# An expert's rows 129 to 192 as 32-row pieces in native fp32 on four column tiles, or as a second tile of 128 rows

## What is computed

```python
logits = (h @ w_router).astype(jnp.float32)
top_logit, top_e = lax.top_k(logits, TOP_K)
gates = jax.nn.softmax(top_logit, axis=-1)
...
def swiglu(h, w1, w3, w2):
    return (jax.nn.silu(h @ w1) * (h @ w3)) @ w2
...
yb = lax.map(expert_block, (xb, block_e)).reshape(n_rows, D)
y = jax.ops.segment_sum(yb * row_gate[:, None], row_tok, num_segments=T + 1)
```

## Time and profile before

| | |
|---|---|
| median of 3 runs | 2439.51 us (2437.66 to 2441.33) |
| profiled execution | 2438.57 us |
| its span | 2436.7 us |
| mean granted TensorE clock | 0.951 |
| TensorE matmul busy | 2242.2 us, 92% |
| VectorE, ScalarE, GpSimd busy | 1483.8, 1089.2, 342.9 us |
| DMA | 512.63 MB, mean 210 GB/s |

### The profile page before, as it was taken

The page is one execution under the profiler, slowest core; times in us unless marked ns, Lnnn a source line. Parts: engine busy times, 40 slices in busy tenths (PEclk is TensorE's granted clock), DMA queues, the critical chain, the costliest instruction groups (busy, mean ns, idle before and its releaser), DMA issues.

```text
span 2436.7 us, 29275 instructions
## 1 busy us (share of the span) xinstructions
PE 2242.2 (92%) x10996; PEld 1824.1 (75%) x10997; DVE 1483.8 (61%) x1330; ACT 1089.2 (45%) x1066; POOL 342.9 (14%) x211
## 2 busy tenths in 40 slices
PE   7999979999996998599899999999999999999990
PEld 4866757887875886578788888888878788888770
DVE  3456565534458444489445454458999995544986
ACT  4145433221323222577334343347777774434761
POOL 0000117888742000100000000000000000000004
PEclk8989989999998998599999999999999999999995
DMA  7420164544431222299554555549999996455963
GB/s 302 183 84 1 51 263 172 185 177 173 172 121 69 104 86 104 84 387 378 221 190 178 188 211 188 199 172 366 365 392 374 383 368 247 173 189 187 360 227 139
DMA packets 76170, 512.63 MB, mean 210 GB/s; under 512 B 8240, under 2 KB 8368, under 8 KB 19024
## 3 DMA queue, kind: packets, MB, share of 16 engines
q1 hardware_dynamic: 61344, 442.46, 47.7%
q0 software_dynamic: 14768, 69.35, 7.8%
HBM read 482.41 MB, written 29.36 MB: 210 GB/s over the span
## 4 chain that ended last, share of the span: by engine, by line
PE 88%; DVE 6%; ACT 2%; DMA 2%; issue 1%; POOL 0%; SPq 0%; POOLq 0%; DVEq 0%; ACTq 0%
PE ps L1509 26%; PE ps L1511 26%; PE ps L1510 26%; PE ps L543 2%; PE ps L498 2%; PE ps L554 2%; PE ps L1778 1%; DMA raw<-w_mod 1%; PE ps L1550 1%; PE ps L502 1%; DVE xz L1149 0%; PE ps L1721 0%; DVE rstd L1143 0%; DVE zf L1480 0%; DVE zf L1485 0%
## 5 line engine op out<-in xcount | busy, mean ns | idle before, releaser
L1509 PE MATMUL ps<-ah,hi 128*128 128x512 f32 x688 | 272.2, 396 | 19.5 <-DVE al L1116 12.9
L1510 PE MATMUL ps<-al,hi 128*128 128x512 f32 x688 | 270.4, 393 | 0.0
L1511 PE MATMUL ps<-ah,lo 128*128 128x512 f32 x688 | 270.2, 393 | 0.0
L1332 DVE TENSOR_TENSOR lob<-raw,hib 128x2048 fp32r<-128x2048 f32 x112 | 251.6, 2282 | 12.3 <-DMA dispatched_x<-ht,di 12.3
L1332 DVE TENSOR_TENSOR loa<-raw,hia 128x2048 fp32r<-128x2048 f32 x112 | 251.0, 2282 | 10.2 <-ACT hia L934 10.2
L1332 DVE TENSOR_TENSOR lo<-raw,hi 128x2048 fp32r<-128x2048 f32 x112 | 255.8, 2284 | 0.0
L1385 DVE TENSOR_TENSOR he<-se,ps 128x512 f32<-128x512 f32 x112 | 76.9, 686 | 290.8 <-ACT se L958 290.4
L1509 PE MATMUL ps<-hia,xth 128*128 128x512 f32 x616 | 246.7, 400 | 4.7 <-issue 4.7
L1509 PE MATMUL ps<-hib,xth 128*128 128x512 f32 x616 | 245.4, 398 | 0.0
L1509 PE MATMUL ps<-hi,hh 128*128 128x512 f32 x616 | 240.5, 390 | 2.2 <-DVE hl L1389 1.5
L1511 PE MATMUL ps<-hia,xtl 128*128 128x512 f32 x616 | 241.5, 392 | 0.0
(11 more groups left out here) (242 smaller groups left out, 3899.4 us busy)
## 6 DMA issues: line engine op xcount, KB each, us to landing
raw<-w_moe SPq DMA_DIRECT2D x336, 1024.0 KB, 6.0
raw<-w_pre SPq DMA_DIRECT2D x59, 1024.0 KB, 4.8
raw<-w_mod POOLq DMA_DIRECT2D x28, 1024.0 KB, 5.1
raw<-w_mod SPq DMA_DIRECT2D x20, 1024.0 KB, 7.0
dispatched_x<-zt POOLq DMA_DIRECT2D x22, 512.0 KB, 14.9
xg<-dispatched_x POOLq DMA_DIRECT2D x8, 1024.0 KB, 7.2
expert_y<-ys POOLq DMA_DIRECT2D x8, 1024.0 KB, 5.4
expert_y<-zt POOLq DMA_DIRECT2D x6, 512.0 KB, 24.4
```

The lines of the kernel that those rows point to most:

```text
L1332: dve.tensor_tensor(LO_OF[j], raw8(r), HI_OF[j].bitcast(F32), ALU.subtract).then_inc(raw_used[r], 1)
L1509: pe.matmul(outp, wh, ah, start=first, stop=False, skip_group_check=True)
L1510: pe.matmul(outp, wh, al, start=False, stop=False, skip_group_check=True)
L1511: return pe.matmul(outp, wl, ah, start=False, stop=last, skip_group_check=True)
```

## The change

An expert with 129 to 160 rows runs its first 128 rows as one tile, and rows 129 to 160 as one piece of 32; an expert with 161 to 192 rows runs one tile and two pieces; 193 to 256 rows take two tiles as before. A piece's products are made in native fp32 from the raw weights and unsplit values: four matmuls, on four tiles of 32 columns of TensorE's array, each take another quarter of the output features with the same 32 rows, so that a piece fills 128 output partitions (4 quarters by 32 rows).

- TensorE: `up`, `turn_hidden` and `down` take a number of pieces, and do their calls ahead of the tile's. The loop over experts covers all eight, reads three values into registers (count, one piece, two pieces) and holds four bodies, each behind a branch of its own. Each body writes two groups out and loops over five, since the counts of the new semaphores begin with the second group.
- SyncE: the raw buffer of a unit used by pieces is free only when TensorE has read it as well. `expert_unit` waits on `FREED` semaphores, four of them, ahead of the loads of units 0, 2, 4 and 5. A body with pieces raises them once in a group, after the pieces' calls; a body without them raises each by 7 at its first use. `WHERE` gives units 2, 3 and 4 other raw slots, so that each pair 0/1 and 2/3 is adjacent.
- ScalarE copies the unsplit hidden values of the 64 piece rows (`HTF`) ahead of `hh`; VectorE copies the unsplit tokens (`XTF`) in `token_tiles`.
- VectorE's routing gets the flags for one and two pieces and a second index table `DIY` for the gather, since the piece rows' results lie elsewhere in `expert_y`.
- GpSimd stores, for every expert, the usual 256 rows and four small blocks with the piece rows' results (whether pieces were run or not), loads token rows once more behind the last expert, and gathers by `DIY`.
- The last expert loads and transposes token rows of a following expert as the others do, and nobody uses them.

```diff
+PIECE = 32
+PIECES = 2
+N_YROWS = N_ROWS + NE * PIECES * PIECE
...
+        RAWP = [put("rawp0", [P, 2, KD, 256], F32, base), put("rawp1", [P, 2, KD, 256], F32, r2 + 16384)]
+        HTF = put("htf", [P, 2, PIECES * PIECE], F32, o_idr)
...
+        XTF = put("xtf", [P, KD, PIECES * PIECE], F32, o)
...
-        WHERE = {0: (0, 0), 1: (1, 1), 5: (2, 5), 2: (3, 3), 3: (4, 4), 4: (5, 2)}
+        WHERE = {0: (0, 0), 1: (1, 1), 5: (2, 5), 4: (3, 2), 2: (4, 3), 3: (5, 4)}
+        RAW_OF = {0: RAWP[0][:, 0], 1: RAWP[0][:, 1], 2: RAWP[1][:, 0], 3: RAWP[1][:, 1], 4: raw8(3), 5: raw8(2)}
+        FREED = {0: up_raw_free[0], 2: up_raw_free[1], 4: down_raw_free[0], 5: down_raw_free[1]}
...
+        LOAD_TURN = {**RAW_TURN, **{("freed", j): 1 for j in FREED}}
...
+            def expert_unit(j, src):
+                if j in FREED:
+                    sp.wait_ge(FREED[j], t.n(("freed", j)))
+                    sp.sem_inc(load_turn, 1)
+                slot = WHERE[j][0]
+                sp.wait_ge(raw_used[slot], t.n(("raw", slot)))
+                sp.dma_start(RAW_OF[j].rearrange("p k n -> p (k n)"), src).then_inc(raw_loaded[slot], 16)
+
             def first_units(at, units):
                 for j in units:
-                    load(WHERE[j][0], unit(at + j))
+                    expert_unit(j, unit(at + j))
 
             def next_units(at):
 
                 for j in (0, 1):
-                    load(WHERE[j][0], unit(at + (6 + j)))
-                load(WHERE[5][0], unit(at + 5))
+                    expert_unit(j, unit(at + (6 + j)))
...
+            first_units(0, (0, 1, 4))
...
+            with t.loop(sp, NE * GROUPS - 1, LOAD_TURN) as g:
...
-            def store(i, n):
+            def store(i, n, landed, pieces):
                 pool.wait_ge(ys_a, n + 1)
                 pool.wait_ge(ys_b, n + 1)
                 pool.sem_inc(pool_turn, 1)
                 pool.dma_start(rows(yg_d, i), YS[:]).then_inc(y_out, 16)
-                pool.wait_ge(y_out, n * 16)
+                if pieces:
+                    at = i * (PIECES * PIECE) + N_ROWS
+                    for c in range(4):
+                        dst = yg_d[bass.ds(at, PIECES * PIECE), c * 256:(c + 1) * 256]
+                        pool.dma_start(dst.rearrange("(a p) n -> p a n", a=PIECES),
+                                       YS[c * PIECE:(c + 1) * PIECE, 1, 0:512].rearrange("p (a n) -> p a n", a=PIECES)
+                                       ).then_inc(y_out, 16)
+                pool.wait_ge(y_out, landed)
                 pool.sem_inc(ys_free, 1)
...
+            with pool.Fori(0, NE) as e:
                 pool.wait_ge(xt_full, e * 4 + 4)
                 pool.sem_inc(pool_turn, 1)
                 pool.dma_start(XG[:], rows(xg_d, e + 1)).then_inc(xg_in, 16)
-                store(e, e + 1)
-            store(NE - 1, NE)
+                store(e, e + 1, e * 80 + 80, True)
...
+                act.activation(HTF[:], PS[:, 2 * q, :].rearrange("p (k n) -> p k n", k=2)[:, :, P:P + PIECES * PIECE],
+                               ACT.Copy)
                 act.activation(HH[:].rearrange("p a n -> p (a n)"), PS[:, 2 * q, :], ACT.Copy).then_inc(hh_ready, 1)
...
+            cnt = RF[:, 0:8]
+            for i, low_end in enumerate((P, P + PIECE)):
+                step(dve.tensor_scalar(SHIFT[:, 0, :], cnt, float(low_end), None, ALU.is_gt))
+                step(dve.tensor_scalar(SHIFT[:, 1, :], cnt, float(low_end + PIECE), None, ALU.is_le))
+                step(dve.tensor_tensor(RF[:, 12 + 8 * i:20 + 8 * i], SHIFT[:, 0, :], SHIFT[:, 1, :], ALU.mult))
+            step(dve.tensor_copy(RI[:], RF[:]))
+            step(dve.tensor_tensor(SHIFT[:, 0, :], RF[:, 12:20], RF[:, 20:28], ALU.add))
+            step(dve.tensor_scalar(SHIFT[:, 1, :], RT[:, 264:272], PIECES * PIECE / CAP - 1.0, float(N_ROWS - P),
+                                   ALU.mult, ALU.add))
+            step(dve.tensor_tensor(SHIFT[:, 0, :], SHIFT[:, 0, :], SHIFT[:, 1, :], ALU.mult))
+            for i in range(4):
+                ins = dve.tensor_tensor(BEYOND[:, i, :], BEYOND[:, i, :], SHIFT[:, 0, :], ALU.mult)
+            step(ins)
+            step(dve.tensor_tensor(PB[:], PB[:], BEYOND[:], ALU.add))
+            for c in range(2):
+                step(dve.tensor_tensor(PT1[:], OH[:, c], PB[:], ALU.mult))
+                step(dve.tensor_reduce(DF[:, c, :], PT1[:], AX.X, ALU.add))
+            step(dve.tensor_copy(DIY[:], DF[:]))
...
+                dve.tensor_copy(XTF[:, 2 * q:2 * q + 2, :],
+                                PS[:, q, :].rearrange("p (k n) -> p k n", k=2)[:, :, P:P + PIECES * PIECE])
...
-            def up(q, tiles, r=None):
+            def up(q, tiles, pieces, r=None, whole=0):
 
                 for j in (2 * q, 2 * q + 1):
                     arrived(j)
+                if whole and not pieces:
+                    pe.sem_inc(up_raw_free[q], whole)
                 hi, lo = ((HIA, LOA), (HIB, LOB))[q]
+                if pieces and r is not None:
+                    pe.wait_ge(xtl_ready, r * 4)
+                for a in range(pieces):
+                    outs = PS[:, 2 * q + 1, :].rearrange("p (h n) -> p h n", h=2)[:, :, 64 * a:64 * a + 64]
+                    for k in range(KD):
+                        for c in range(4):
+                            at = slice(c * PIECE, (c + 1) * PIECE)
+                            ins = pe.matmul(outs[at], XTF[:, k, a * PIECE:(a + 1) * PIECE],
+                                            RAWP[q][:, :, k, 64 * c:64 * c + 64], start=(k == 0), stop=(k == KD - 1),
+                                            skip_group_check=True, tile_position=(0, c * PIECE))
+                if pieces:
+                    ins.then_inc(up_raw_free[q], 1)
                 ks = [k for i in XT_ORDER for k in (2 * i, 2 * i + 1)] if r is not None else list(range(KD))
                 for s in range(tiles):
                     cols_ = slice(s * P, (s + 1) * P)
@@ -1770,21 +1840,40 @@
                                     hi[:, :, k, :], lo[:, :, k, :], i == 0, i == KD - 1)
                 ins.then_inc(up_done[q], 1)
 
-            def turn_hidden(q, tiles):
+            def turn_hidden(q, tiles, pieces):
 
                 pe.wait_ge(he_ready, t.n("he"))
+                for a in range(pieces):
+                    for c in range(4):
+                        to = slice(64 * (c % 2), 64 * (c % 2) + 64)
+                        col = (c // 2) * CAP + P + a * PIECE
+                        pe.matmul(PS[to, 2 * q, col:col + PIECE], HE[:, 1, 64 * a:64 * a + 64],
+                                  ident[:, c * PIECE:(c + 1) * PIECE], start=True, stop=True, skip_group_check=True,
+                                  tile_position=(0, 64 * (c % 2)))
                 for k in range(2):
                     for s in range(tiles):
                         ins = pe.transpose(PS[:, 2 * q, k * CAP + s * P:k * CAP + (s + 1) * P],
                                            HE[:, s, k * P:(k + 1) * P], ident)
                 ins.then_inc(ht_full, 1)
 
-            def down(q, tiles, first=False):
+            def down(q, tiles, pieces, first=False, whole=0):
 
                 arrived(4 + q)
+                if whole and not pieces:
+                    pe.sem_inc(down_raw_free[q], whole)
                 pe.wait_ge(hl_ready, t.n("hl"))
                 hi = (HI[2], HI5)[q][:].rearrange("p (k n) -> p k n", k=2)
                 lo = (LO[2], LO5)[q][:].rearrange("p (k n) -> p k n", k=2)
+                raw = RAW[WHERE[4 + q][0]][:].rearrange("p (k n) -> p k n", k=2)
+                for a in range(pieces):
+                    for k in range(2):
+                        for c in range(4):
+                            at = slice(c * PIECE, (c + 1) * PIECE)
+                            ins = pe.matmul(PS[at, 6, 256 * a:256 * a + 256], HTF[:, k, a * PIECE:(a + 1) * PIECE],
+                                            raw[:, k, 256 * c:256 * c + 256], start=(first and a == 0 and k == 0),
+                                            stop=True, skip_group_check=True, tile_position=(0, c * PIECE))
+                if pieces:
+                    ins.then_inc(down_raw_free[q], 1)
                 for k in range(2):
                     for s in range(tiles):
                         cols_ = slice(s * P, (s + 1) * P)
@@ -1797,52 +1886,63 @@
             turn = {("raw", r): 1 for r in range(6)}
             turn.update({"he": 2, "hl": 2})
 
-            def expert(tiles, r, more):
-
-                up(0, tiles, r)
-                turn_hidden(0, tiles)
-                up(1, tiles)
+            def expert(tiles, pieces, r, following=True):
+
+                rows_ = (tiles, pieces)
+                up(0, *rows_, r, whole=GROUPS)
+                turn_hidden(0, *rows_)
+                up(1, *rows_, whole=GROUPS)
                 pe.wait_ge(ys_a, r)
                 pe.wait_ge(ys_b, r)
-                down(0, tiles, True)
-                turn_hidden(1, tiles)
```

(74 more changed lines are left out.)

39 lines of the change are left out of this document (23 added, 16 removed).

## The result

The changed kernel takes 2506.5 us (median; 2502.5 to 2509.7) where the kernel before takes 2440.4 beside it: a ratio of 1.027 (95% interval 1.026 to 1.029), so slower, by 66 us. The forecast was 2490, with a range of 2400 to 2570. The profiled execution has a span of 2500.9 us against 2436.7.

A forecast was written before the change was run, and what follows sets the result against it. TensorE, busy 92% of the span, was taken as the bound. From 2438.6 us, pieces -82, jumps +130 and tail +3 gave 2489.6; with the median 0.9 above, 2490 us, range 2400 to 2570.

The forecast's parts named there:

- pieces: Experts 1 and 6: pieces replace the second tile, 7.7 us a group for one, 13.6 for two; gain 82 us.
- boundaries: Between experts: jumps over four long bodies wait for code, +130 us over seven boundaries, bounds +92 and +183.
- tail: After the last expert: four small stores delay gathering, +2 us, and skipped bodies add three misses, +1.
- the 0.109 us for a step of four column tiles: Up products of a piece: 16 steps at 0.109 us, twice, 3.5 us a group; bounds 0.109 and 0.22 a step.
- rival 3: Up steps take 0.22 us, so piece pairs cost more than the tile in expert 6: 2563 us, chance 0.12.
- The 3 us that I took off for the token parts: Experts 1 and 6: the first up product waits for all four token parts, about 1.5 us back each.
- + 144: Expert loop: all four jumps of an expert wait, 21.7 us a boundary, seven boundaries, less the 7.7 paid before.
- Rivals 1 and 2: Code once run stays: 2378 us, chance 0.17; or half stays, some 12 misses: 2420 us, chance 0.17.
- rival 2: Expert loop: half the code stays where neighbours in time take the same body, some 12 misses: 2420 us, chance 0.17.
- the 3.4 us of lead: Expert boundaries: TensorE's sequencer runs 3.4 us ahead of its matmuls, taken off each boundary's waits.
- the slow clock: Behind each standstill: matmuls at the 1.2 GHz level, 0.43 us apart against 0.227, adding 3.0 us a boundary.
- Late loads: One-tile experts: SyncE's new waits make load 5 0 to 2 us late, covered by the standstill in the forecast.

The follow-up runs named there:

- one_body: Changed kernel with one body for all experts, pieces and second tile behind small branches in each stage: 2499.9 us, ratio 1.025 to the kernel before.
- nested_skip: Changed kernel with the three bodies for over 128 rows inside one further branch, same code size: 2417.0 us, ratio 0.990 to the kernel before.
- dead_body_2: Kernel before plus two never-run bodies equal to the two-tile one, about 2,350 instructions in the loop: 2595.6 us, ratio 1.064.
- dead_body_1: Kernel before plus one never-run body equal to the two-tile one, about 1,700 instructions in the loop: 2448.5 us, ratio 1.004.
- tree_small: Changed kernel with its branches as a tree and two written groups a body instead of three: 2395.2 us, ratio 0.982 to the kernel before.
- rest_only: Changed kernel without pieces and their bodies, all SyncE's counts raised behind an expert's first up product: 2457.0 us, ratio 1.007 to the kernel before.
- credit_ahead: `rest_only` with SyncE's four counts starting 7 higher, so loads never wait for TensorE's first up product: 2439.5 us, ratio 1.0006 to the kernel before.
- no_pieces: Changed kernel with both piece flags always zero, so experts 1 and 6 run two tiles: 2591.5 us, ratio 1.063 to the kernel before.

## Why the prediction was right, point by point

- **Sign and size.** 2490 forecast, 2506.5 measured. By stretches from one result's copy to the next: pieces - 88 (forecast - 82), boundaries + 149 (+ 130; what the stretches grow by beyond the pieces), tail + 6 (+ 3), start of the experts - 3 (not forecast): + 64, the difference of the spans.
- **Pieces.** The up product of one piece takes 1.95 us as one row, switch included (1.74 forecast, plus the switch), the down product 1.07 (0.9, plus the switch): the 0.109 us for a step of four column tiles was right, so rival 3 is out, and 7.65 us a group stands against 7.7. Two pieces cost 13.25 a group, 13.6 forecast. The 3 us that I took off for the token parts don't show: both experts begin with a standstill that "issue" ends, which is long enough to cover them. The sequencer kept up but for 0.39 us in expert 1 and 1.57 in expert 6, both in the first run of pieces behind the standstill; `one_body` has more of this.
- **Jumps.** I took 3 to 4 waits at each boundary and weighed them as + 130 between + 115 and + 144. All 28 came, and four more behind the last expert. They are spread from one to six at a boundary, not four each: each expert skips three bodies, some ahead of its own and some behind it, which I had overlooked and which leaves the sum as it is; the mean is 4.80 us where I had 4.66. The + 144 that "all wait" gives is 5 short of the 149. The mis-sized step is this choice of 3.5 for 4. Rivals 1 and 2 fall for this kernel, but rival 2's idea, that neighbours of one body keep their code, is what `nested_skip` shows as soon as fewer ends are touched; I had no row on how much stays. The forecast's reason, that a loop of 5,800 instructions is too long to stay, holds only in its effect: `nested_skip` has the same 5,800, and what counts is how much of them a turn touches.
- **Why they wait.** The prediction left open whether length or distance counts. The Trainium skill ("Runtime: NRT & Kernel Launch", "Instruction fetch mechanics") says that a taken branch out of the current two-page window waits for a fetch; by that rule all waits of the changed kernel follow, but the 0.2 us of `nested_skip` over 5,800 instructions contradict it. Its other figure, 2,048 instructions in blocks of 256 for TensorE, makes eight blocks, and the two dead bodies agree with it: a one-tile turn of `dead_body_2` brings nine packets, one more than eight, each time; with one target and its two packets fewer, `dead_body_1` would need seven by my estimate, and it brings none between 1780 and 2020.
- **Lead and clock.** The jumps at the end of expert 3 began at 1760.0 and the matmuls ended at 1763.4: the 3.4 us of lead again. Behind the standstill the records are at the 1.2 GHz level as in the earlier trace rows and change to 0.23 us from 1786.8 on, after 2.8 us. The other boundaries stay there for 4.6 to 7.7 us. By half of each length (my estimate) the slow clock costs 1.4 to 3.9 us a boundary, about 19 in all, where I had 3.0 each, 21; the seven standstills add up to 134.8 us, where four waits each gave 7 x 18.7 = 131.
- **Late loads.** I had them at 0 to 2 us an expert and covered by the standstill. Covered, yes: in the changed kernel experts 4 and 5 show none, and only experts 0, with none ahead of it, and 3, where it is 2.9 us, do, 0.8 us each. Where the cover is gone, `nested_skip` shows 0.7 us in expert 0 and 1.7 to 2.4 in experts 3, 4 and 5, `tree_small` 0.8 and 2.1 to 2.5: my bound of 2 was a little short. The 4.4 to 4.7 of `rest_only` belong to its counts, which come 2.5 us later than those of the change.
- **The tail.** + 6 for + 3. The number hides two errors. Gathering starts 11.0 us after the last large store's issue, 8.5 before, which looks like the + 2 forecast for the four small stores. But `rest_only`, `credit_ahead` and `nested_skip` issue the same stores and gather 8.2, 8.4 and 8.8 us after: the small stores alone cost nothing. Only `no_pieces`, which also has four slow branches there, shows such a delay (10.8); how the branches delay it stays open, since `dead_body_2`, with slow branches and none of the small stores, has 8.3. The slow branches themselves I had hidden beside that wait. They aren't: TensorE's last block begins after 15.8 us of idle time where it was 11.5, since the last of four slow branches ahead of it (4.1 us from 2444.0 on) ends at 2448.1, later than VectorE's part that it used to wait for. In `nested_skip`, with one slow branch there, the tail is back within 0.6 us, and in `dead_body_2` it is 4.6 us longer than before without any small store.

The tail's rows, TensorE's and GpSimd's of the changed kernel, then GpSimd's large store and first gather of `rest_only`:

```profile
2448.19 1.22 PE L1950 MATMUL ps<-dg,small 128*128 128x128 f32 x4 [15.82 <-issue]
...
2444.99 1.00 POOL L784 DMA_INDIRECT yg<-expert_y,diy  x1 [7.13 <-issue]
```

```profile
2397.44 0.72 POOL L755 DMA_DIRECT2D expert_y<-ys  x1 [107.39 <-DVE ys L1459]
...
2405.69 1.00 POOL L784 DMA_INDIRECT yg<-expert_y,diy  x1 [4.33 <-issue]
```

## What to carry to other kernels

Before adding a special body to a loop, count what one turn touches of an engine's instructions, the ends of skipped bodies included, and read in the trace how long a branch to code not yet run takes; a saving of a few us a group can be lost to four such branches a turn, as here. Put rare bodies behind one common branch: with the expert counts of this input, that alone moved this change from 2.7% slower to 1.0% faster, and a tree with shorter bodies to 1.8%. How often each body runs, and next to which, decides what its code costs. And a wait that costs nothing beside a standstill must be priced again in the version that removes the standstill.

## What the runs showed of the hardware that I had not expected

- Where every turn takes the same way, code is kept whole or not at all: from one one-tile expert to the next one more skipped end takes the skip branches from 0.2 us to between 5.5 and 6.6 (`dead_body_1`, `dead_body_2`). The branches of the group loop inside a body stay at 0.2.
- Distance doesn't matter: 0.2 us for a jump back over some 5,800 instructions (`nested_skip`).
- Straight code of small matmuls can be faster than its own delivery: 3.5 us of standstill in the middle of 64 records (`one_body`).
